# Hyena convolution in a transformer block, spectral stage: products in place, and a three-buffer ring of whole-group stores in place of two half-group buffers

## What is computed

```python
s = v * x1
y = irfft(rfft(s, n=2*L) * rfft(g, n=2*L))[:L]
y = (y + s * skip) * x0
```

## Time and profile before

| what | value |
|---|---|
| median of 3 runs | 2643.86 us (2642.76 to 2653.99) |
| the profiled execution: span, first to last instruction | 2636.2 us |
| what lies around the span, against the median | 7.7 us |
| PE busy | 2482.3 us, 94% |
| DVE / ACT / POOL busy | 44% / 25% / 27% |
| chain that ended last, PE's share | 70%, by far the most in the panel matmuls (L1060) |
| spectral stage, first `ga` copy to last store's issue | 447.2 to 631.3 us |
| `inv` stage, PE's first matmul to the first of the next stage | 635.3 to 674.7 us |
| DMA busy, mean over 16 engines, whole span | 25% |

### The profile page before, as it was taken

How to read it: one execution, slowest core, us unless ns; L and a number is a source line. 1 busy time by engine, 2 the same in 40 slices (tenths; PEclk the granted TensorE clock), 3 DMA queues, 4 the chain that set the end, 5 groups by cost and what they waited for, 6 DMA issues and landing times.

```text
span 2636.2 us, 29935 instructions
## 1 busy us (share of the span) xinstructions
PE 2482.3 (94%) x11420; PEld 1987.5 (75%) x11420; DVE 1164.5 (44%) x1221; ACT 661.1 (25%) x816; POOL 702.4 (27%) x394
## 2 busy tenths in 40 slices
PE   7987998777999999999999889999999999999996
PEld 5775665444788888888888679888888787778885
DVE  7899564332623321331234693626262322430443
ACT  4102345344411000010012262626363101111011
POOL 2233111331232333333333312222212232233331
PEclk9998999898999999999999899999999999999998
DMA  5232215876011111111111120202011421111231
GB/s 190 73 127 88 80 64 209 162 169 146 24 48 48 48 48 48 48 49 52 66 48 48 56 96 25 72 24 72 27 69 47 187 90 59 64 40 57 95 120 72
DMA packets 61099, 208.06 MB, mean 79 GB/s; under 512 B 6182, under 2 KB 7848, under 8 KB 60906
## 3 DMA queue, kind: packets, MB, share of 16 engines
q1 hardware_dynamic: 46090, 161.02, 18.8%
q10 hardware_dynamic: 14944, 46.14, 5.9%
HBM read 162.05 MB, written 36.70 MB: 75 GB/s over the span
## 4 chain that ended last, share of the span: by engine, by line
PE 70%; DVE 3%; ACT 1%; issue 0%; ACTq 0%; DVEq 0%
PE ps L1060 59%; PE ps L468 4%; DVE T L1687 1%; PE ps L1290 1%; PE ps L515 1%; PE ps L534 1%; PE ps L497 1%; PE ps L536 1%; PE ps L535 1%; PE ps L1082 0%; DVE XN L1717 0%; PE ps L1091 0%; DVE X L1997 0%; DVE H L1710 0%; PE ps L439 0%; DVE T L1717 0%
## 5 line engine op out<-in xcount | busy, mean ns | idle before, releaser
L1060 PE MATMUL ps<-H,whi 128*128 128x512 f32 x4000 | 1086.3, 394 | 32.9 <-POOL wlo L1016 14.0
L1060 PEld LDWEIGHTS ps<-H,whi 128*128 128x128 f32 x4000 | 752.6, 189 | 204.9 <-issue 23.7
L1014 POOL CAST whi<-wraw 128x1024 fp32r<-128x1024 f32 x190 | 201.5, 1060 | 1808.2 <-issue 738.8
L1060 PE MATMUL ps<-H,wlo 128*128 128x512 f32 x2000 | 619.3, 391 | 0.0
L1016 POOL TENSOR_TENSOR wlo<-wraw,whi 128x1024 fp32r<-128x1024 f32 x194 | 489.0, 2521 | 58.5 <-ACT whi L602 43.3
L1060 PEld LDWEIGHTS ps<-H,wlo 128*128 128x128 f32 x2000 | 377.2, 189 | 79.3
L1060 PE MATMUL ps<-A,whi 128*128 128x512 f32 x1472 | 395.6, 391 | 6.4 <-DVE A L2029 4.9
L1060 PEld LDWEIGHTS ps<-A,whi 128*128 128x128 f32 x1472 | 277.0, 189 | 65.0 <-issue 5.3
L1060 PE MATMUL ps<-A,wlo 128*128 128x512 f32 x736 | 227.0, 390 | 0.0
L1060 PEld LDWEIGHTS ps<-A,wlo 128*128 128x128 f32 x736 | 138.6, 188 | 28.9
L1946 DVE TENSOR_TENSOR T<-ps,T 128x1024 f32<-128x1024 f32 x22 | 26.9, 1224 | 202.6 <-PE ps L1060 202.6
(11 more groups left out here) (342 smaller groups left out, 2614.3 us busy)
## 6 DMA issues: line engine op xcount, KB each, us to landing
wraw<-in_panels SPq DMA_DIRECT2D x181, 512.0 KB, 3.4
mw<-in_modp SPq DMA_DIRECT2D x24, 512.0 KB, 3.5
g<-gsp ACTq DMA_DIRECT2D x16, 512.0 KB, 2.6
wraw<-g SPq DMA_DIRECT2D x16, 512.0 KB, 11.1
s<-sa SPq DMA_DIRECT2D x16, 512.0 KB, 2.6
bs<-s SPq DMA_DIRECT2D x16, 512.0 KB, 7.8
YB<-yi ACTq DMA_DIRECT2D x32, 256.0 KB
kf<-in_kfft SPq DMA_DIRECT2D x16, 320.0 KB, 8.2
```

Of the source, the lines that this page charges most:

```text
L1014: nc.gpsimd.tensor_copy(whi[:, s, :, :], wraw[:, s, :, :]).then_inc(hi_made, 1)
L1060: last = mm(p[:, c * step:(c + 1) * step], w[:, ws, k, :], operand(act, a, k, c * step, step), start=(q == 0 and w is whi and a == 0), sto ...
```

## The change

Four things are done.

1. DVE writes the products into `ga` and `gb` themselves; `ya` and `yb` are gone. PE's inverse reads `ga` and `gb`. DVE's wait for `spec_inv` goes, and ACT, ahead of the copy into `ga` for step `n`, waits for `spec_inv >= n - 1` (the inverse of step n - 2) where it waited for `spec_y`.
2. `yi` becomes three buffers of 128 x 1024 values, for a whole group each.
3. The store is one per group: 128 rows of 4 KB, 512 KB, issued after the second half's copy. ACT waits for a free buffer once per group, for the store of three groups before.
4. The `inv` stage waits for all stores ahead of its first job, on PE and also on ACT, ahead of `skip_of(0)`, since T0 and T1 now lie under `yi`.

```diff
-        ya = [at(f"ya{u}", [P, 512], RT + 2 * K * u) for u in range(2)]
-        yb = [at(f"yb{u}", [P, 512], RT + 4 * K + 2 * K * u) for u in range(2)]
-        yi = [at(f"yi{u}", [P, 512], RT + 12 * K + 2 * K * u) for u in range(2)]
+        yi = [at(f"yi{u}", [P, T], RT + (0, 4, 12)[u] * K) for u in range(3)]
...
-        yb_in = [sem("yb_in0"), sem("yb_in1")]
+        yb_in = [sem(f"yb_in{u}") for u in range(3)]
+
+        def yb_full(eng):
+            for u in range(3):
+                eng.wait_ge(yb_in[u], 16 * len(range(u, GROUPS, 3)))
...
-                for q, (m, src) in enumerate(((3, ya), (4, yb))):
+                for q, (m, src) in enumerate(((3, ga), (4, gb))):
...
-                    if m0 == 0:
-                        pe.wait_ge(yb_in[c0 // 512], 16 * GROUPS)
+                    if o == 0:
+                        yb_full(pe)
...
             def spec_inverse(n):
-                c = n % 2
+                g, c = n // 2, n % 2
                 act.wait_ge(spec_inv, n + 1)
-                if n >= 2:
-                    act.wait_ge(yb_in[c], 16 * (n // 2))
-                A_(yi[c][:, :], ps[2 * c + 1][:, 512:1024], ACT.Copy).then_inc(spec_ev, 1)
-                act.wait_ge(spec_ev, n + 1)
-
-                act.dma_start(YB[8 * (n // 2):8 * (n // 2) + 8, :, 512 * c:512 * c + 512], yi[c][:, :]
-                              ).then_inc(yb_in[c], 16)
+                if c == 0 and g >= 3:
+                    act.wait_ge(yb_in[g % 3], 16 * (g // 3))
+                A_(yi[g % 3][:, 512 * c:512 * c + 512], ps[2 * c + 1][:, 512:1024], ACT.Copy).then_inc(spec_ev, 1)
+                if c:
+                    act.wait_ge(spec_ev, n + 1)
+                    act.dma_start(YB[8 * g:8 * g + 8, :, :], yi[g % 3][:, :]).then_inc(yb_in[g % 3], 16)
...
                 if n >= 2:
-                    act.wait_ge(spec_y, 2 * n - 2)
+                    act.wait_ge(spec_inv, n - 1)
...
+            yb_full(act)
             skip_of(0)
...
                 dve.wait_ge(spec_xm, n + 1)
-                if n >= 2:
-                    dve.wait_ge(spec_inv, n - 1)
-                for q, (t, gg) in enumerate(((ya, ga), (yb, gb))):
+                for q, gg in enumerate((ga, gb)):
                     dve.wait_ge(spec_g, 2 * n + q + 1)
-                    V_.tensor_tensor(t[c][:, :], ps[2 * c][:, 0:512], gg[c][:, :], ALU.mult).then_inc(spec_y, 1)
+                    V_.tensor_tensor(gg[c][:, :], ps[2 * c][:, 0:512], gg[c][:, :], ALU.mult).then_inc(spec_y, 1)
```

## The result

The changed kernel takes 2673.78 us (median of 4 runs, 2670.77 to 2676.89), beside 2644.36 for the kernel before (4 runs, 2642.76 to 2653.99): the ratio is 1.0107 [1.0090, 1.0124], so it is **29 us slower**. The profiled execution took 2676.89 us with a span of 2675.1. I forecast 2632.9 and a range of 2614 to 2655; the time lies outside, on the side to which I gave 0.09.

A forecast was written before the change was run, and what follows sets the result against it. The store's flow was taken to bound the stage: 459.5 + 16 x 10.2 us per group + 1.6 puts `inv` at 624.3 against 635.3, 11.0 us less, so 2632.9 us; range 2614 to 2655.

The forecast's parts named there:

- What bounds the stage: Stage before `inv`: the store holds `yi`, ACT, DVE and PE follow; eight nearly full DMA engines carry it at 55 GB/s.
- Products in place: DVE's products written into `ga` and `gb`: ACT's new wait is covered by PE's order, cost 0.
- `skip_of` behind the wait: ACT's 2.19 us at the start of `inv` now begin when PE begins: 0, up to 0.5 us.
- Half the issues: ACT drops 16 store issues of 0.62 us, 10 us in all, on an engine idle longer: 0 on the path.
- 4 KB rows: Store packets halve, bytes stay: 0, with ends of -1.4 and up to +3.4 us per group.
- The ring of three: Three `yi` buffers close the gaps without store bytes: a group's period becomes 10.2 us, between 9.5 and 10.9.
- Start and end: First store issued at 458.26 instead of 454.38 us; last store must land whole, PE starting `inv` 1.6 us after its last bytes.
- SP's queue: The 4 MB load of `X` runs beside the last stores, counted like the missing group loads: 0, bounds 0 to +3 us.
- The second: Rival, chance 0.08: load packets wait behind 4 KB store packets, a group takes 12.6 us, 27 us slower, 2671.
- The third: Rival, chance 0.20: the eight engines are full, periods stay 12.0 and 11.0 us, late start shows as +10 us, 2654.
- The first: Rival, chance 0.25: fixed cost per store goes, a group takes 9.1 us, 28.6 us less, 2615.

The follow-up runs named there:

- the spread runs: Stores sent to 8 target partitions four or two apart instead of neighbours, in the changed kernel, its variants and the kernel before: 2581.10 to 2608.47 us.
- the early ring: Changed kernel with its three buffers, but each half group stored at once in 2 KB rows (32 stores): 2647.39 us (1.0012), again 2650.98 us (1.0008).
- The pair of late and early: Changed kernel with 2 KB row stores, two issued together after the second half (2670.45 us) or each half stored at once (2650.98 us).
- the spread target alone: Changed kernel with each group's store going to 8 partitions four apart instead of neighbours, matrix rows permuted to match: 2588.24 us, 0.9793.

## Why the prediction was wrong, point by point

- **What bounds the stage: right.** The store's flow, not the compute engines nor the number of buffers, sets the pace; the spread runs show it from the other side. That exactly eight engines carry a store stays a reading of the small packets; no run changed their number.
- **Products in place, 0: right** (1.0007). **`skip_of` behind the wait, 0: right**; ACT's copy of the results comes 3.7 us after PE starts, 3.4 before. **Half the issues, 0, and 4 KB rows, 0: right** together: one store of 4 KB rows or two of 2 KB rows at the same moment, 2670.92 and 2670.45.
- **The ring of three, the first step that failed: 10.2 us a group, 11 us gained in all; by itself it gains 0** (1.0012 and 1.0008). I wrote that ACT would run ahead, fill the ring and wait for the store of three groups before, at 10.2 us a group from rates measured with stores alone and with few loads beside. It never filled the ring. Loads and stores share the engines that are full, and a buffer makes neither of them faster: the stores' 71.8 us of waiting became the loads' 63.6. My period was bounded by 9.5 and 10.9, from stretches of a few microseconds in the steady half; measured, in the same form, it is 12.7. Over 480 to 600 us the stores move 5.48 MB before, 5.14 in the early ring and 4.81 in the change. The step from 5.48 to 5.14 is not clear of the scatter between executions (the two-buffer kernel with the products in place has 5.16 in its trace); the step to 4.81 goes with the late issue. I had seen that the loads "will share, and slow the stores", but took this for a brake on a gain, with no change as the worst case.
- **Start and end, the second step that failed: the moment of issue is worth 20 us, not 3.9.** I counted that the first store leaves 3.9 us later and put the late issue of every other group at nothing, without a reason. The pair of late and early shows it, 2670.45 and 2650.98. Half of the bytes leave a half group later, each time; in the traces 10 us or more of the difference come after the first store.
- **SP's queue: X at 0.** As the sum uses it, right: beside `X` the stores flow at 41 GB/s, 12.8 us for a group, as beside the loads of the loop (12.7). What I missed is that the stores of the drain could have gone at 60 with nothing beside them: the load's place costs 5 to 8 us in the three versions in which it was tried, all of which wait for all stores before `inv`.
- **The rivals.** The second, with a chance of 0.08, had the number (2671), the place (`kh` waits for `kf`) and the period (12.6, found 12.7). Its *mechanism*, load packets behind long store packets, fell as the cause of the loss: 4 KB and 2 KB rows take the same time. The waits do follow the row length at the short end (`kf` 36.8 us with 1 KB rows, 67.2 with 2 KB), but the time doesn't. So its number was luck. "A starved loop makes no stores and the backlog drains", my argument against it, describes the cycle above, but brought no relief in time. The third, "eight engines are full, nothing is gained" (2654), is what the early ring does. Its tail into slower was where more of my chance belonged: with the engines over 100% by my own count, a gain of any size needed bytes that go faster, and no part of the change makes them so. The first fell: 16 stores fewer gave nothing back. With it falls the estimate that I drew from the Trainium skill ("DMA: Bandwidth & Descriptors", "Anatomy of one DMA"), up to 32 us. The section gives its 2 us for DMAs that GpSimd issues, and the stores here are ACT's; with 16 stores or 32, issued at the same moments, the time is the same (2670.92 and 2670.45).

**Still open:** why stores that are issued a half group later flow more slowly. That they cost 20 us is shown; the cycle of stalls and the late start don't explain it. Whether a smaller backlog would help was not tested.

## What to carry to other kernels

Where a transfer's flow is the limit, more buffers only hand the wait to the next transfer on the same engines: ask first what holds the flow. Here a target of a few neighbouring partitions did, and permuting it cost nothing. Don't join stores to save issues if that makes the first bytes wait, and keep a large load that nobody needs yet out of the drain. After an experiment that adds a wait, check in the trace that the wait ever held.

## What the runs showed of the hardware that was not expected

- A store into few partitions slows transfers that don't touch them: with the spread target alone, `kf` lands in 5.4 us instead of 11.9 and `wraw` in 8.0 instead of 14.8.
- Rows of 1, 2 and 4 KB make no difference to the time on this path (2646.54, 2647.39; and late 2670.45, 2670.92).
- The same kernel, the changed one, showed a drain of 29.4 us in one profiled execution and 19.5 in another, with times of 2676.89 and 2669.48: of the 7.4 us between them, the drain (9.9) accounts for more than all. The flow in it was about the same, 41 and 38 GB/s beside `X`; what differed was the bytes left when the loop ended, 1.11 and 0.70 MB. One profiled execution is not enough to price a drain.
